# TensorE's eight expert passes of a mixture-of-experts block, written out one behind the other

## The chip, the cores and the metric

One Trainium2 chip, one core of it. The metric is the device time of one execution in microseconds; the time before is the median of three runs. The numbers of the profile come from one further execution, taken by the hardware profiler.

## The reference

Two small transformers stand one behind the other, in f32, on 256 tokens of width 1024 (and 256 context tokens beside them). The first has two hybrid layers (two kinds of attention and a convolution), the second a differential-attention layer with a dense feed-forward part, and then a Fourier-mixing layer with a mixture of experts. The change lies in that last part alone:

```python
def swiglu(h, w1, w3, w2):
    return (jax.nn.silu(h @ w1) * (h @ w3)) @ w2

def moe_swiglu(h, router, w1, w3, w2):          # 8 experts, D = 1024, D_FF = 3584
    logits = (h @ router).astype(jnp.float32)
    top_v, top_i = lax.top_k(logits, TOP_K)     # TOP_K = 2
    gates = jax.nn.softmax(top_v, axis=-1)
    ...                                         # rows sorted by expert
    def expert_block(args):
        xe, e = args
        return swiglu(xe, w1[e], w3[e], w2[e])
    yb = lax.map(expert_block, (xb, block_e))
    ...                                         # gated rows added up per token
```

Each expert has three f32 matrices of 1024 x 3584 numbers, 44 MB together, and is given the tokens that chose it.

## The kernel before

The kernel is written engine by engine, with semaphores set by hand: `block.sync` issues the loads, `block.tensor` the matmuls, `block.scalar` and `block.vector` work on what the matmuls leave in the eight banks of PSUM, `block.gpsimd` gathers and scatters rows by index. Everything before the experts (about the first 1,110 us) is straight code on every engine.

The experts are done in passes. A pass takes up to 96 tokens (`SLOTS`) of one expert. There are always eight passes, one for each expert, and up to five more (`OVER`) where an expert was chosen by more than 96 tokens. A list made on the chip (`LIST`) holds the number of all passes and of the extra ones. TensorE, ScalarE, VectorE and GpSimd each read the number of passes from it into a register (for TensorE line 1360) and run a loop of that many turns: lines 1362 (TensorE), 1882 (ScalarE), 2543 (VectorE), 727 (GpSimd). SyncE's loop over the eight experts (line 695) is separate from its loop over extra passes, which stands behind a test of `extra`.

A pass of TensorE consists of 24 chunks of weights in the order of `moe_order()`. The `up` chunks multiply the pass's tokens (`HE`, held in the memory of `modrow`) by columns of w1 or w3, and the `down` chunks multiply the hidden values by rows of w2. The order is: w1 first half, four chunks; `select(5)`, a small product that draws the rows of the next pass; w3 first half, four; w1 second half, four, with the transposes `turn_hidden(0)` after its second; `down(0, 0)` and `down(0, 1)`; w3 second half, four; `down(0, 2)`, `turn_hidden(1)`, `down(0, 3)`; `turn_tokens()`, which transposes the tokens of the next pass; and `down(1, 0)` to `down(1, 3)`. Nearly all products go through the helper `product`, so the profile puts them on its line, L757; the transposes are L1406 and L1416. One product of the source shows as two matmuls and two weight loads in the trace: a pass has 1,473 matmuls.

Chunks lie in a ring of eight slots in SBUF, 2 MB for a chunk of the first half and 1.5 MB for one of the second. SyncE loads a chunk (line 693) once TensorE has released its slot: `weights_used` is raised on the last matmul that reads the old chunk, or on one soon after it. TensorE waits for `weights_landed` before it reads a chunk (line 1370). It also waits for ScalarE and VectorE at places: before an `up` group for its bank (line 1388), before `select` for `pick_ready` (line 1441). That one is raised by VectorE (lines 2546 to 2555) at each pass's head: it waits until the last pass's result rows are scattered to DRAM (line 2548 behind GpSimd's line 735), and then makes the selection `PICK` for the next pass.

Every wait in the loop counts against the turn number `j`, as in

```python
pe.wait_ge(weights_landed[s], j * 48 + (landed_base[s] + 16 * (turn + 1)))
```

so the value waited for is worked out in a register in each turn. After the loop nothing is left for TensorE; ScalarE, VectorE and GpSimd then store the last result rows, fetch the two rows of each token, add them and apply the last norm.

Of the kernel before, what the change touches and what calls it, by code (L numbers as in the profile page):

```python
# [61 lines left out]
EXPERTS = 8  # L62
SLOTS = 96
GROUPS = SLOTS // 32
OVER = 5
# [133 lines left out]
def build(nc, a, table, out, dumps=None):  # L199
    chunks = weight_chunks(a)  # L200
    index = {}
    for i, (name, _) in enumerate(chunks):
        index.setdefault(name, []).append(i)
# [15 lines left out]
    for i, (_, parts) in enumerate(chunks):  # L219
        earlier.append(loads[slots[i]])  # L220
        loads[slots[i]] += 1
        total[slots[i]] += 16 * len(parts)
        landed_at.append(total[slots[i]])
    moe_slots = list(range(RING, LATE_SLOT)) + sorted(used_last, key=used_last.get) + [LATE_SLOT]

    with ExitStack() as ctx:
        def sb(name, shape, dt=F32):
            return ctx.enter_context(nc.sbuf_tensor(name, shape, dt))
# [146 lines left out]
        LIST = sb("LIST", [1, 32], I32)  # L375
        L_PASSES, L_EXTRA, L_OFFSET = 14, 15, 16
# [165 lines left out]
        def spec_columns(specs):  # L542

            at, c = [], 0
            for _, _, nb, n in specs:
                at.append(c)
                c += nb * (n // P)
            return at, c
# [3 lines left out]
        def moe_order():  # L552

            up = [[(w, st, q) for q in range(4)] for st in range(2) for w in ("w1", "w3")]
            down = [[("w2", st, q) for q in range(4)] for st in range(2)]
            return up[0] + up[1] + up[2] + down[0][:2] + up[3] + down[0][2:] + down[1]
# [191 lines left out]
        def _(pe):  # L748
# [424 lines left out]
            for what, u in attention_steps(2 * DA_HEADS, FILL[2]):  # L1173
# [3 lines left out]
                elif what == "scores":  # L1177
                    for i in range(2):
                        b, _ = start()
                        r = slice(64 * i, 64 * i + 64)  # L1180
# [176 lines left out]
            for primed in (silu_done, turned_ready, turned_taken, down_taken):  # L1357
                pe.sem_inc(primed, 3)
            pe.wait_ge(list_ready, 1)
            passes = pe.value_load(LIST[0:1, L_PASSES:L_PASSES + 1], min_val=EXPERTS, max_val=EXPERTS + OVER)  # L1360

            with pe.Fori(0, passes) as j:
                order = iter(enumerate(moe_order()))

                def moe_chunk(kind, st, q):
# [54 lines left out]
                def down(st, q):  # L1420

                    s, w = moe_chunk("w2", st, q)
                    rows = (4, 3)[st]
                    turned = HIDDEN_T[st]
                    if q == 0:
                        pe.wait_ge(turned_taken, j * 6 + (3 * st + 6))
                    for i in range(rows):
                        first, last = (st, q, i) == (0, 0, 0), (st, q, i) == (1, 3, rows - 1)

                        def part(g):  # L1430
                            return turned[:, q, i, 32 * g:32 * g + 32] if q < GROUPS else turned[:, g, i, SLOTS:P]

                        for r in range(GROUPS):
                            dst = bank[6 + r // 2][:, LAT * (r % 2):LAT * (r % 2) + LAT]
                            m = tiles(dst, part, part(r), w[:, i, :], LAT * r, LAT * GROUPS, first and r != 1,
                                      last and r != 0)
                    m.then_inc(weights_used[s], 1)
# [18 lines left out]
                for q in range(4):  # L1456
                    down(1, q)
                assert not release
            turn_log["pe"] = t.g


# [1164 lines left out]
```

## Time and profile before

| | |
|---|---|
| median of 3 runs | 2101.5 us (2100.93 to 2102.09) |
| the profiled execution's own time | 2105.07 us |
| its span, first to last instruction | 2103.2 us |
| mean granted TensorE clock in it | 0.965 |
| busy share: matmuls (PE) / weight loads (PEld) | 94% / 58% |
| busy share: VectorE / ScalarE / GpSimd | 35% / 27% / 1% |
| chain that ended last | PE 87%, DVE 5%, issue 3%, DMA 2%, ACT 2% |
| read from HBM / written | 535.19 MB / 5.25 MB |

Times in the profile are microseconds from the span's start. "Issue" is time in which an engine waited for nothing that the profile shows. PEq, DVEq and so on are an engine's sequencer, which handles branches, register arithmetic and waits and hands the rest on to the engine. Matmuls overlap each other, so their single durations are longer than the distance from one to the next. A granted clock of 1.00 is 2.4 GHz and one of 0.50 is 1.2 GHz.

### The profile page before, as it was taken

The numbers are of one execution on the slowest core, as the hardware profiler recorded it, in microseconds if no ns is written. First come the engines' busy times: TensorE is split into PE (matmuls) and PEld (weight loads), VectorE is DVE, ScalarE is ACT, GpSimd is POOL, SyncE is SP. The second block draws the span as 40 slices with busy tenths as digits, with TensorE's granted clock in tenths as the row PEclk, the third lists the DMA queues.
The fourth block names the chain that finished last, engine by engine and source line by source line (L and its number), as shares of the span: only waits on it lengthen the run. The fifth ranks groups of instructions, "written<-read, shape, count | busy, mean of one in ns | idle before, by whom it ended". The sixth has DMA issues, their size and how long they took to land.

```text
span 2103.2 us, 41141 instructions
## 1 busy us (share of the span) xinstructions
PE 1981.8 (94%) x18171; PEld 1218.5 (58%) x18171; DVE 736.7 (35%) x1419; ACT 576.4 (27%) x1062; POOL 27.6 (1%) x42
## 2 busy tenths in 40 slices
PE   6999998999899989999999989899999989999995
PEld 4785577866688467888873534435353443435343
DVE  4862756856744567665560000000000000000002
ACT  3233544444431555554440000000000000000001
POOL 1000000000000000000000000000000000000000
PEclk8999999999899999999999999999999999999998
DMA  9202522255632855566696999999999999989991
GB/s 328 83 33 99 201 81 67 101 202 189 250 120 81 322 186 212 181 204 181 230 382 242 393 348 374 387 341 411 332 395 347 376 380 352 409 329 393 349 370 69
DMA packets 179828, 543.29 MB, mean 258 GB/s; under 512 B 6778, under 2 KB 42257, under 8 KB 163132
## 3 DMA queue, kind: packets, MB, share of 16 engines
q1 hardware_dynamic: 175776, 528.63, 67.5%
q0 software_dynamic: 3104, 9.59, 1.3%
q8 instruction: 161, 2.64, 0.5%
q10 hardware_dynamic: 764, 2.24, 0.3%
q14 instruction: 23, 0.19, 0.0%
HBM read 535.19 MB, written 5.25 MB: 257 GB/s over the span
## 4 chain that ended last, share of the span: by engine, by line
PE 87%; DVE 5%; issue 3%; DMA 2%; ACT 2%; SPq 1%; POOL 0%; ACTq 0%; DVEq 0%; POOLq 0%; PEldq 0%
PE bank L757 82%; PE bank L795 2%; PE bank L1406 1%; DMA ring<-in_w_mod 1%; DVE ring_r L2104 1%; PE bank L866 1%; DMA ring<-in_ada_w 1%; SPq L686 1%; DVE nmax L2141 0%; PE bank L1070 0%; DVE H L2024 0%; DVE H_r L2033 0%; PE bank L827 0%; DVE H L2053 0%; ACT ring_r L1575 0%
## 5 line engine op out<-in xcount | busy, mean ns | idle before, releaser
L757 PE MATMUL bank<-scratch,modrow 128*32 128x384 f32 (+1 forms) x3840 | 380.5, 547 | 42.2 <-issue 42.0
L757 PE MATMUL bank<-H_r,ring_r 128*128 128x256 f32 (+2 forms) x1296 | 300.9, 314 | 1.4 <-ACT H_r L1486 1.4
L757 PEld LDWEIGHTS bank<-scratch,modrow 128*32 128x32 f32 x3840 | 130.9, 112 | 282.3 <-issue 282.3
L757 PE MATMUL bank<-scratch_r,ring_r 128*128 128x256 f32 (+2 forms) x1280 | 277.4, 344 | 5.6 <-ACT scratch_r L1559 2.1
L757 PE MATMUL bank<-ring,modrow 128*32 128x512 f32 (+1 forms) x2304 | 238.4, 557 | 0.0
L757 PEld LDWEIGHTS bank<-scratch_r,ring_r 128*128 128x128 f32 (+1 forms) x1280 | 216.4, 195 | 35.9 <-issue 4.6
L757 PEld LDWEIGHTS bank<-H_r,ring_r 128*128 128x128 f32 (+1 forms) x1296 | 222.9, 188 | 18.5 <-ACT H_r L1486 1.3
L757 PE MATMUL bank<-ring,scratch 128*32 128x256 f32 (+1 forms) x4048 | 228.0, 380 | 0.0
L2565 DVE TENSOR_TENSOR H<-H,bank 128x512 f32<-128x512 f32 (+1 forms) x48 | 29.8, 621 | 483.6 <-PE bank L757 483.6
L757 PE MATMUL bank<-H_r,scratch_r 128*128 128x512 f32 x544 | 192.7, 400 | 0.9 <-DVE H_r L2044 0.5
L757 PE MATMUL bank<-scratch 128*32 128x256 f32 (+5 forms) x2160 | 190.4, 370 | 2.8 <-ACT scratch L1481 1.8
L757 PEld LDWEIGHTS bank<-ring,scratch 128*32 128x32 f32 (+1 forms) x4048 | 132.3, 110 | 91.0 <-issue 6.0
L757 PEld LDWEIGHTS bank<-ring,modrow 128*32 128x32 f32 x2304 | 77.0, 110 | 143.9 <-issue 142.4
L1896 ACT ACTIVATE scratch<-bank 128x512 f32<-128x512 f32 (+1 forms) x48 | 22.6, 545 | 479.0 <-PE bank L1406 479.0
L757 PEld LDWEIGHTS bank<-scratch 128*32 128x32 f32 (+4 forms) x2160 | 109.7, 129 | 60.5 <-issue 31.2
L1481 ACT ACTIVATE scratch<-bank 128x512 f32<-128x512 f32 (+5 forms) x135 | 69.8, 530 | 194.3 <-PE bank L757 145.6
L757 PEld LDWEIGHTS bank<-H_r,scratch_r 128*128 128x128 f32 x544 | 102.8, 189 | 27.2 <-DVE H_r L2044 2.4
L2117 DVE TENSOR_TENSOR ring_r<-ring,scratch_r 128x2048 fp32r<-128x2048 f32 (+1 forms) x47 | 103.4, 2201 | 41.8 <-ACT scratch_r L1583 40.3
L2104 DVE TENSOR_TENSOR ring_r<-ring,ring_r 128x2048 fp32r<-128x2048 f32 (+2 forms) x42 | 92.4, 2200 | 25.1 <-ACT ring_r L1575 24.2
L1583 ACT ACTIVATE scratch_r<-ring 128x2048 fp32r<-128x2048 f32 (+1 forms) x47 | 86.1, 1836 | 41.6 <-PE bank L757 40.6
L1889 ACT ACTIVATE H<-bank 128x512 f32<-128x512 f32 (+1 forms) x48 | 26.1, 544 | 253.1 <-PE bank L757 253.1
L1575 ACT ACTIVATE ring_r<-ring 128x2048 fp32r<-128x2048 f32 (+2 forms) x42 | 77.3, 1841 | 60.7 <-PE bank L757 58.9
(249 smaller groups left out, 1692.4 us busy)
## 6 DMA issues: line engine op xcount, KB each, us to landing
ring<-in_moe_w SPq DMA_DIRECT2D x56, 2048.0 KB, 10.6
scratch<-in_moe_w SPq DMA_DIRECT2D x56, 1536.0 KB, 8.0
scratch<-in_moe_w SPq DMA_DIRECT2D x40, 2048.0 KB, 11.1
ring<-in_moe_w SPq DMA_DIRECT2D x40, 1536.0 KB, 9.3
ring<-in_ada_w SPq DMA_DIRECT2D x24, 2048.0 KB, 9.7
ring<-in_ff_w SPq DMA_DIRECT2D x14, 2048.0 KB, 7.8
ring<-in_w_mod SPq DMA_DIRECT2D x12, 2048.0 KB, 11.7
ring<-in_ff_w SPq DMA_DIRECT2D x8, 1792.0 KB, 8.2
```

What stands on the lines that cost most here:

```text
L686: sp.dma_start(dst, src).then_inc(weights_landed[s], 16)
L757: m = nc.tensor.matmul(out_, w, x_, start=first, stop=last)
L795: m = nc.tensor.transpose(dst, src, ident[0:n, 0:n])
L866: last = nc.tensor.matmul(bank[b][m * h:m * h + m, P * tt:P * tt + P], root[:, 3, c:c + 1].broadcast_to([P, m]), ident, start=True, stop=True)
L1481: nc.scalar.activation(dst, src, func, **kw).then_inc(bank_taken[b], 1)
L1575: nc.scalar.activation(high1(n), raw1(n, ring), ACT.Copy).then_inc(hi_ready, 1)
L1583: nc.scalar.activation(ff_high(n), ff_half(n, ring), ACT.Copy).then_inc(hi_ready, 1)
L1889: nc.scalar.activation(SIL[:, r, 0:WIDE[st]], bank[r][:, 0:WIDE[st]], ACT.Silu)\
L1896: nc.scalar.activation(HIDDEN_T[st][:, r, :, :], bank[3 + r][:, 0:WIDE[st]].rearrange("p (i s) -> p i s", s=P), ACT.Copy).then_inc(turned_ ...
L2104: v.tensor_tensor(raw1(n, ring_r), raw1(n, ring), high1(n).bitcast(F32), ALU.subtract)\
L2117: v.tensor_tensor(ff_half(n, ring_r), ff_half(n, ring), ff_high(n).bitcast(F32), ALU.subtract)\
L2565: v.tensor_tensor(HIDDEN[:, r, 0:WIDE[st]], SIL[:, r, 0:WIDE[st]], bank[3 + r][:, 0:WIDE[st]], ALU.mult).then_inc(mult_done, 1)
```

## The change

The body of TensorE's loop becomes a function `expert_pass(j)`. It is called eight times with the whole numbers 0 to 7, so that eight copies of the body stand one behind the other and the values waited for are constants. A ninth copy stands in a loop over the extra passes with `j = r + 8`, behind a test `extra > 0`. What is loaded into the register at line 1360 is now the number of extra passes. The inputs here give eight passes and no extra one. No matmul, no order and no wait's value is changed, and the other engines keep their loops.

```diff
             pe.wait_ge(list_ready, 1)
-            passes = pe.value_load(LIST[0:1, L_PASSES:L_PASSES + 1], min_val=EXPERTS, max_val=EXPERTS + OVER)
-
-            with pe.Fori(0, passes) as j:
+            extra = pe.value_load(LIST[0:1, L_EXTRA:L_EXTRA + 1], min_val=0, max_val=OVER)
+
+            def expert_pass(j):
+
                 order = iter(enumerate(moe_order()))
...
                 for q in range(4):
                     down(1, q)
                 assert not release
+
+            for e in range(EXPERTS):
+                expert_pass(e)
+            with pe.If(extra > 0):
+                with pe.Fori(0, extra) as r:
+                    expert_pass(r + EXPERTS)
+                pe.nop()
             turn_log["pe"] = t.g
```

## Rows read from the trace of the kernel before

**Rows 1.** The page: busy time by engine.
```profile
PE 1981.8 (94%) x18171; PEld 1218.5 (58%) x18171; DVE 736.7 (35%) x1419; ACT 576.4 (27%) x1062; POOL 27.6 (1%) x42
```

**Rows 2.** Waits of PE, 1110.3 to 2078.5 us: total us, times, longest us.
```profile
PE bank L757 <- issue: 42.0, 12, 5.3
```

**Rows 3.** The chain that ended last, in order of time: start us, us, what.
```profile
1110.60 51.30 PE bank L757 x484
...
1225.20 5.27 issue
1230.47 4.16 PE bank L757 x22
1234.63 1.33 issue
1235.96 47.95 PE bank L757 x462
...
1347.21 5.18 issue
...
1967.08 47.99 PE bank L757 x462
...
2078.41 0.02 issue
```

**Rows 4.** Sequencer, lines L1362, L1882, L1370, L1388: ns min/median/max, first and last start.
```profile
L1362 PEldq COMPARE_BRANCH  x8: 83/6082/6267, 1223.8 to 2077.0; - x8
...
L1882 ACTq COMPARE_BRANCH  x8: 40/45/59, 1225.3 to 2078.5; - x8
...
L1370 PEldq ALU_OP  x72: 32/32/32, 1125.1 to 2069.1; - x72
...
L1388 PEldq ALU_OP  x40: 32/32/42, 1110.7 to 2007.8; - x40
```

**Rows 5.** DMA queues, packets and MB: first 1225.2 to 1230.5 us, then 1230.5 to 1347.2.
```profile
DMA packets 285, 2.21 MB, mean 417 GB/s; under 512 B 16, under 2 KB 16, under 8 KB 16
q8 instruction: 1, 0.02, 1.3%
...
DMA packets 8022, 42.89 MB, mean 367 GB/s; under 512 B 400, under 2 KB 400, under 8 KB 6224
q8 instruction: 13, 0.21, 0.7%
```

**Rows 6.** Stretches: us, busy us (x) of PE, PEld, DVE, ACT, POOL, clock, DMA share, GB/s.
```profile
1595.90:1601.00 5.10, 5.07 (x22) 1.01 (x23) 0.00 (x0) 0.00 (x0) 0.00 (x0) 0.50 1.02 415
1602.00:1712.80 110.80, 110.80 (x1451) 49.55 (x1443) 4.62 (x12) 6.96 (x14) 0.92 (x1) 1.00 0.95 364
806.60:1096.80 290.20, 287.31 (x1732) 245.35 (x1730) 190.03 (x310) 151.66 (x233) 1.09 (x2) 1.00 0.67 226
1270.00:1347.00 77.00, 77.00 (x1145) 38.63 (x1137) 3.73 (x6) 5.17 (x11) 0.00 (x0) 1.00 1.01 398
```

**Rows 7.** Weight loads in order of time, start us and us of each four.
```profile
1236.39 0.15 PEld L757 LDWEIGHTS bank<-scratch,modrow 128*32 128x32 f32 x4 [0.27 <-issue]
1236.82 0.16 PEld L757 LDWEIGHTS bank<-scratch,modrow 128*32 128x32 f32 x4 [0.27 <-issue]
```

**Rows 8.** SyncE's waits, 1110 to 2079 us; landing of its loads, line L693.
```profile
SPq L693 <- PE bank L757: 857.2, 184, 31.9
...
DMA to landing us min/median/max: 6.2/9.6/23.6
```

**Rows 9.** VectorE in order of time at the second pass's head.
```profile
1236.92 0.15 DVE L2548 CAST result_row<-slot_next 96x1 int32<-96x1 f32 x1 [9.77 <-DMA result_rows<-scratch,result_row]
...
1238.88 0.16 DVE L2555 COPY of_slot<-of_expert 128x4 f32 x1
1255.47 0.15 DVE L2558 CAST slot_row<-bank 96x1 int32<-96x1 f32 x1 [16.43 <-PE bank L757]
```

## The prediction

> **What bounds the kernel now.** I read the page first. Matmuls are busy for 94% of the span, and no other engine for more than 35% [rows 1], so TensorE is the bound. From 1,110 us on there is nothing but the eight passes and, after 2078.41, a tail of 2103.2 - 2078.4 = 24.8 us in which TensorE does nothing [rows 3]. The question is then what TensorE waits for inside the passes. The list of its waits has one entry there: 42.0 us in 12 waits, the longest 5.3, and all for "issue", which is no semaphore, no other engine and no DMA [rows 2]. The chain of waits says where. A pass ends at 1225.20, TensorE stands for 5.27 us, runs 22 matmuls in 4.16 us, stands again for 1.33 us, and then goes through the pass with no further stop to 1347.21, where the next stall of 5.18 us begins [rows 3]. So the stall stands at the end of each turn of the loop, seven times in all. The end of the last pass, 2078.41, sets when the tail can begin.
>
> The stall has an owner. The loop's branch, line L1362, took 83 ns in one of its eight turns, the last (its start, 2077.0, is just before the last matmul), and about 6.1 us in the others, up to 6.27; the branches of ScalarE's loop took 40 to 59 ns [rows 4]. A branch that is not taken, and one in a short loop, cost next to nothing; a taken one in TensorE's long loop costs 6 us. The first begins at 1223.8, 1.4 us before the pass's end at 1225.20, because the sequencer runs ahead, so about 5 us of it are seen. The queues tell why: during the stall there is one packet of instructions (0.02 MB), and in the pass after it there are 13 with 0.21 MB, so 16 KB each [rows 5]. The body is fetched anew in every turn, and after the jump back TensorE has nothing to do until the first block is there. The 1.33 us after 22 matmuls have the look of the wait for the second block.
>
> **Skill and row.** The row says 6.1 us for a taken branch and 0.08 for the one not taken [rows 4]. The Trainium skill, "Advanced Engine Details and Errata", section Control Flow Timing, gives about 108 ns for a compare-and-branch, with no word of where it goes. By that figure seven branches would be worth 0.8 us in all and the change nothing; by the row each is worth fifty times as much. It is the second rival below, on a price of its own.
>
> **What the change removes.** *The seven jumps back.* Between one pass's last matmul and the next one's first there is now only the following instruction. I count what is lost at a turn as a whole, since the restart costs too: the clock. In 1595.9 to 1601 the granted clock is 0.50 (1.2 GHz), right behind such a stall, and 1.00 from 1602 to the pass's end [rows 6]. At 1.00 four matmuls of this kind start every 1236.82 - 1236.39 = 0.43 us, 0.107 each [rows 7], so 22 of them take 2.35 us where the turn shown needed 4.16 and then stood for 1.33.
> A pass from its 23rd matmul to its end takes 1347.21 - 1235.96 = 111.25 us, and in the last turn 2078.41 - 1967.08 = 111.33 [rows 3]. A pass with no stop in front is then 2.35 + 111.25 = 113.60. The seven passes after the first took 2078.41 - 1225.20 = 853.21 us with their stalls [rows 3]; written out they take 7 x 113.60 = 795.2. The difference is **58.0 us**. As a check, the shown turn lost 5.27 + 4.16 + 1.33 - 2.35 = 8.41, and the mean is 58.0 / 7 = 8.29. Of it some 5.1 is the branch and 3.2 the slow restart. The first pass (1110.60 to 1225.20 [rows 3]) is entered from straight code as before: 0.
>
> *The register arithmetic of the waits.* It runs in the sequencer ahead of the array, and a pass has no stop from it of its own [rows 2, 3]. I take 0. Nothing is added to the waits, so there is no loss. The most it could give back: lines L1370 and L1388 show 72 + 40 register operations of 32 ns in eight passes [rows 4], 14 a pass or 0.45 us; I allow 0.7 us a pass for these and the few of other waits, 8 x 0.7 = 5.6.
>
> **What it adds.** *The seam.* A pass's first matmuls wait for tokens, banks and a landed chunk; all have been raised before the pass ends, or the chain would show them behind the stall instead of issue [rows 3]. I take 0. The upper bound is 1 us at each of seven seams, an allowance for a short stop that the stall now hides. *The test for extra passes.* It jumps over a ninth body, once, so up to 6.27 us [rows 4]; it lies behind TensorE's last matmul and under the tail of 24.8 us, which does not use TensorE. With that cover gone it would cost 6.3. *The longer program.* Eight bodies are fetched once each instead of one body eight times: 13 packets a pass either way [rows 5].
>
> **What is late next.** Weights. A pass moves 2.21 + 42.89 = 45.1 MB [rows 5] in 121.9 us now, 370 GB/s, and in 113.6 it needs 397. The stretch 1270 to 1347, in which TensorE runs with no stop, has just that, 398 GB/s, and no wait for a load; in the stall 417 are moved [rows 5, 6]. SyncE is not behind: 184 of its loads in this part waited for TensorE to release a slot [rows 8]. A slot is loaded again about 8 of 24 chunks before its use, 8/24 of 113.6 = 38 us less the 5 us of the chunk itself; landing takes 9.6 us in the median and 23.6 at worst [rows 8]. That leaves 10 to 23 us. Next VectorE's selection for the following pass: it is done at 1239.04, 13.8 us after the pass's end, nearly all of it waiting for the scatter of result rows, and does not depend on TensorE's stall [rows 9]. TensorE's select ran just before VectorE's 1255.47 [rows 9], some 19 us after the 23rd matmul; written out it comes about 19 + 2.35 = 21.3 us after the old pass's end. The margin shrinks from 16 to 7.5 us. Both hold, so I cost them at 0, and they carry the first rival.
>
> **Sum.** The profiled execution: 2105.07 - 58.0 = 2047.1. It lies 3.6 us above the median of the runs, and nothing in the sum depends on that, so the forecast for the median is 2101.5 - 58.0 = **2043.5 us**. Its own bounds: 7 seams at 1 us above, and 5.6 us of register arithmetic below: 2037.9 to 2050.5.
>
> **Rivals.**
> 1. *The loads or the scatter become the wait.* For it: only 20 GB/s lie between what is needed and the most that is shown, and the stall now gives the queues a rest. Against: the 77 us at 398 GB/s. If the queues held 385 GB/s on average, a pass would be 45.1 / 385 = 117.1 us, 3.5 more, and 7 of them 25: 2068. Where VectorE's wait for the scatter took 10 us more than its 9.8, the cost would be 2.5 us a pass, 2061.
> 2. *The branch is cheap, and the stall has another cause that stays* (the next pass's operands, say). Then the seven branches are worth 0.083 us each [rows 4], 0.6 in all: 2100.9. By the page of the skill named above it would be this case. Against it: the branch's own duration holds the stall, and the one not taken has none [rows 4].
> 3. *The stop goes, the slow restart stays*, for instance by a second block that comes late at the seam. Then only the branches' 7 x 5.1 = 36 us go: 2065.5. Against: with no stop the clock has no cause to fall, and it stayed at 1.00 for 290 us of nearly unbroken matmuls before the passes [rows 6].
> 4. *Slower: straight code outruns its fetch.* If in the loop some of the 13 blocks were at hand from the turn before, written-out passes would stop at every block they now lack, 5.1 us each. The change then loses from 58.0 / (8 x 5.1) = 1.4 missed blocks a pass on; three a pass cost 8 x 3 x 5.1 = 122 us less 58: 2166. Against: the pass from 1110.60 was the first, with nothing at hand, and shows no stop; and 13 packets in a later pass are as many as 1,473 matmuls and as many weight loads fill, so none were kept [rows 3, 5].
>
> **How the numbers follow.** The forecast 0.86; rival 1 0.06; rival 3 0.04; rival 2 0.02; rival 4 0.02. No change that can be told is within 0.2%, 4.2 us, which only rival 2 gives; all of 1 and 3 is faster. So faster 0.96, same 0.02, slower 0.02. The range takes the forecast's own bounds, 2037.9 to 2050.5, a little outwards (the two readings of a pass differ by 0.08 us, 0.6 in seven, and the runs before spread over 1.2): 2036 and 2051. With 0.86 for the case and a little outside its bounds, that leaves out no more than 2 in 10; the other cases lie outside it.
>
> **What would show it.** In the chain of waits the 5 us "issue" entries at the passes' ends are gone, and passes follow each other at 113.6 us; TensorE's last matmul ends near 2020.4. The list of TensorE's waits keeps some 2 us of issue in this part. The granted clock is 1.00 from the first pass's start-up to the end. Instruction packets remain at 12 or 13 a pass. A wait of TensorE for a load or for VectorE's of_slot would show rival 1; a clock of 0.50 or a stop shortly after a seam rival 3; issue stops in mid-pass rival 4; an unchanged stop at the seams with another owner rival 2.

## The result, and the profile after

The changed kernel takes 2043.59 us (median of four runs, 2041.20 to 2045.51) against 2101.80 us for the kernel before beside it (2100.93 to 2105.25): a ratio of 0.9719, 95% interval 0.9705 to 0.9733. The forecast was 2043.5. The profiled execution took 2045.29 us, with a span of 2043.5.

The chain of waits of the changed kernel, in order of time (start us, us, what), shows two seams as nothing at all:

```profile
1112.23 1.50 issue
1113.73 51.41 PE bank L757 x484
...
1212.76 65.19 PE bank L757 x772
1277.95 1.46 PE bank L1407 x12
...
1325.57 65.19 PE bank L757 x772
1390.76 1.46 PE bank L1407 x12
...
2018.13 0.02 issue
```

The 288 matmuls that end a pass and the 484 that begin the next are now one piece, 772 matmuls in 65.19 us. Before they were 15.7 us, a stall of 5, 22 matmuls, a second stop and the other 462 [rows 3]. The same place of two successive passes (1277.95 and 1390.76) is 112.81 us apart; before it was 121.9 in the mean.

TensorE's waits from the first pass to the last (us in total, times, longest), against 42.0 us before [rows 2]:

```profile
PE bank L757 <- issue: 2.0, 1, 2.0
```

It is the stop ahead of the first pass. The branch at the passes' end is gone, and the test for extra passes, line L1463, took 3.8 us. It starts 1.5 us before TensorE's last matmul ends and lies under the tail for the rest:

```profile
L1463 PEldq COMPARE_BRANCH  x1: 3788/3788/3788, 2016.6 to 2016.6; - x1
```

The stretches (us, busy us of PE, PEld, DVE, ACT, POOL, granted clock, DMA share, GB/s) answer to [rows 6]:

```profile
1114.00:1117.40 3.40, 3.40 (x20) 1.08 (x16) 0.53 (x3) 0.00 (x0) 0.00 (x0) 0.50 0.02 5
1117.40:2018.00 900.60, 900.60 (x11768) 398.44 (x11760) 48.71 (x120) 72.62 (x140) 13.82 (x15) 1.00 0.96 381
```

The clock is 0.50 at the first pass's head and then 1.00 for 900 us of unbroken matmuls. DMA queues of one period, 1228.4 to 1341.2 us, the wait of SyncE's loads, and their landing time answer to [rows 5, 8]:

```profile
DMA packets 8305, 45.06 MB, mean 399 GB/s; under 512 B 416, under 2 KB 416, under 8 KB 6240
...
q8 instruction: 11, 0.18, 0.6%
```
```profile
SPq L693 <- PE bank L757: 793.5, 184, 31.7
```
```profile
DMA to landing us min/median/max: 6.3/10.8/23.8
```

The instruction packets are now 11 to 12 a pass, where the loop had 13 and one more at the turn. Loads land a little later (median 10.8 us, 9.6 before), and TensorE waits for none. VectorE's selection at the second pass's head answers to [rows 9]:

```profile
1241.88 0.17 DVE L2563 COPY of_slot<-of_expert 128x4 f32 x1
1249.51 0.15 DVE L2566 CAST slot_row<-bank 96x1 int32<-96x1 f32 x1 [7.46 <-PE bank L757]
```

The margin between the finished selection and the row that follows TensorE's select has gone from 16.4 to 7.5 us.

**Where the time came from.** The two profiled executions differ by 2105.07 - 2045.29 = 59.8 us. From the first matmul of the passes to the last it was 2078.41 - 1110.60 = 967.8 us and is 2018.13 - 1113.73 = 904.4: 63.4 less. The part ahead of the passes was 3.1 us longer in this execution, and the tail 0.5 (25.3 for 24.8): 63.4 - 3.1 - 0.5 = 59.8.

### The profile page after: what moved, and what is told of

Its sections match the earlier page's. It is cut to its first block, busy times and chain, and to the rows that moved or that the text cites. A ratio compares the mean times of both kernels' runs of the same rounds, so it can differ in the third digit from the quotient of the medians.

```text
span 2043.5 us, 40941 instructions
## 1 busy us (share of the span) xinstructions
PE 1960.7 (96%) x18171; PEld 1213.8 (59%) x18171; DVE 737.0 (36%) x1419; ACT 576.5 (28%) x1062; POOL 27.5 (1%) x42
## 4 chain that ended last, share of the span: by engine, by line
PE 89%; DVE 5%; DMA 2%; ACT 2%; issue 1%; SPq 1%; POOL 0%; ACTq 0%; DVEq 0%; POOLq 0%; PEldq 0%
PE bank L757 83%; PE bank L795 2%; PE bank L1407 1%; DMA ring<-in_w_mod 1%; PE bank L866 1%; DVE ring_r L2112 1%; DMA ring<-in_ada_w 1%; DVE nmax L2149 1%; SPq L686 1%; PE bank L1070 1%; DVE H L2032 0%; DVE H_r L2041 0%; PE bank L827 0%; ACT ring_r L1583 0%; DVE scratch L1999 0%
## 5 line engine op out<-in xcount | busy, mean ns | idle before, releaser
L757 PE MATMUL bank<-scratch,modrow 128*32 128x384 f32 (+1 forms) x3840 | 358.3, 531 | 2.0 <-issue 2.0
L757 PEld LDWEIGHTS bank<-scratch,modrow 128*32 128x32 f32 x3840 | 125.3, 110 | 224.5 <-issue 223.3
L757 PE MATMUL bank<-ring,modrow 128*32 128x512 f32 (+1 forms) x2304 | 232.8, 557 | 0.0
L2578 DVE SCALAR_TENSOR_TENSOR scratch<-bank,slot_gate,X 96x512 f32<-96x512 f32 (+1 forms) x16 | 9.1, 610 | 219.3 <-PE bank L757 219.3
## 6 DMA issues: line engine op xcount, KB each, us to landing
ring<-in_w_mod SPq DMA_DIRECT2D x12, 2048.0 KB, 11.7
```

Of the source, the lines that this page charges most:

```text
L757: m = nc.tensor.matmul(out_, w, x_, start=first, stop=last)
```

## The experiments

Each is an edit of the changed kernel. The theory is that a jump back over a body which TensorE no longer holds costs a fetch, and then a restart. Rivals are the register arithmetic of the waits, and any taken branch on TensorE.

### Four turns of two bodies

```diff
-            for e in range(EXPERTS):
-                expert_pass(e)
+            with pe.Fori(0, EXPERTS // 2) as pair:
+                expert_pass(pair * 2)
+                expert_pass(pair * 2 + 1)
```

Expected: 

> TensorE's passes in a loop of four turns with two bodies each, in place of eight bodies: three taken jumps back instead of seven or none. If each taken jump back over a long body costs its stall and restart (63.4 us less in the passes for seven jumps, 9.1 each, or 8.3 by the working of the prediction), the time is 25 to 27 us above the straight kernel, 2068.5 to 2071. If the gain came from constants in place of register values (this kernel still waits on register values in every pass), it stays near the kernel before, 2101. If a longer body makes the stall longer, over 2075.

Measured: 2070.14 us (2068.27 to 2070.26), ratio to the kernel before 0.9843, 0.9829 to 0.9856. The three turns are all that TensorE waits for, and they look like the old ones. Chain, then the branch's row:

```profile
1335.67 5.98 issue
1341.66 5.34 PE bank L757 x22
1347.00 0.09 issue
...
1442.66 65.19 PE bank L757 x772
```
```profile
L1461 PEldq COMPARE_BRANCH  x4: 83/6872/7067, 1334.3 to 2041.2; - x4
```

The seam inside the body (the 772 matmuls from 1442.66) costs nothing, with register values in every wait. In the trace the places where such a piece of 772 begins are 235.5, 235.4 and 236.0 us apart, which is 9.8 to 10.4 us more than two straight passes (2 x 112.81). The time agrees: it is 27.6 us above the next experiment's 2042.56, which has register values and no jump, or 9.2 a jump, and 29.3 above the straight kernel's 2040.88 (below, from another group of runs), or 9.8. The looped kernel lost 63.4 / 7 = 9.1 a jump. The branch itself was 0.8 us longer here (6.87 for 6.08), so the loss goes with the number of jumps, with a slightly dearer stall whose cause is open.

### Register values with no jump

```diff
+            zero = pe.value_load(LIST[0:1, 0:1], min_val=0, max_val=EXPERTS - 1)
...
-                expert_pass(e)
+                expert_pass(zero + e)
```

Expected: 

> Eight bodies written out, but each pass's number is a register (a zero loaded once, plus a constant), so that all waits are again against values worked out in registers, with no jump. Theory of the jump: no change against the straight kernel, 2043.6 within 1 us, plus the one load of some 0.5 us before the passes. Rival, the register arithmetic was what made a warm pass 113.6 us where it is now 112.8: 0.8 us a pass more, 2049 to 2050, with passes 113.6 us apart in the chain.

Measured: 2042.56 us (2041.68 to 2047.40), ratio 0.9720, 0.9707 to 0.9733. The register operations are back and the passes do not feel them. Line L1373 (L1370 in [rows 4]), then the chain:

```profile
L1373 PEldq ALU_OP  x72: 32/32/32, 1125.8 to 2006.3; - x72
```
```profile
1275.37 1.46 PE bank L1409 x12
...
1322.99 65.19 PE bank L757 x772
1388.18 1.46 PE bank L1409 x12
```

1388.18 - 1275.37 = 112.81 us again. The register arithmetic is worth nothing, and it is not what made the prediction's pass 113.6 us.

### A near jump back at every seam

```diff
             for e in range(EXPERTS):
+                if e:
+                    with pe.Fori(0, 2):
+                        pe.nop()
                 expert_pass(e)
```

Expected: 

> Eight bodies written out, and at each of the seven seams a loop of two turns around one empty instruction: seven taken jumps back on TensorE, over a body of a few instructions. Theory of the far jump: 0.1 us of sequencer time each, hidden by the queue in front of the array, 2043.6 within 1 us, and the branch's row shows under 0.1 us. Rival, any taken jump on TensorE throws the fetched instructions away: 5 to 8 us each, 2079 to 2102.

Measured: 2039.78 us (2036.22 to 2041.42), ratio 0.9699, 0.9686 to 0.9713; passes again 112.81 us apart. Seven of the 14 branches below are taken, and none took over 0.26 us (under 0.1 was expected):

```profile
L1463 PEldq COMPARE_BRANCH  x14: 76/145/253, 1220.8 to 1898.0; - x14
```

A taken jump by itself costs TensorE nothing here. So it is the far one.

### How far is far: bodies of growing length

A first try with empty instructions (`pe.nop()`) as the filling settled nothing.

Expected: 

> The straight kernel, and behind its passes on TensorE six loops of three turns over 128, 448, 960, 1,472, 1,984 and 2,496 empty instructions, so that each loop's own branch can be read. If what counts is the distance jumped back against what TensorE still holds, the branch costs under 0.1 us up to some length and about 4 to 6 us (3.8 in the last branch of the straight kernel, with quiet queues) from there on, with the edge between 448 and 2,496. If every jump back of more than a block of 256 costs, 448 and longer all show it. The total time is not compared.

The loop over "2,496" of them took as long as that over "128": the three branches of each start some 0.4 us apart, so nothing stood in the bodies. (Its one run took 2038.88 us.) The branches of the "2,496":

```profile
L1477 PEldq COMPARE_BRANCH  x3: 76/207/213, 2019.7 to 2020.4; - x3
```

The second try used matmuls of four columns:

```diff
+            def filler():
+                nc.tensor.matmul(bank[3][:, 0:4], ident, tab[:, T_ONES:T_ONES + 4], start=True, stop=True)
+
+            with pe.Fori(0, 3):
+                for _ in range(32): filler()
...
+            with pe.Fori(0, 3):
+                for _ in range(624): filler()
```

Expected: 

> The empty instructions of the last try of this kind left nothing in the program. Now six loops of three turns over 32, 112, 240, 368, 496 and 624 small matmuls stand behind the passes, each matmul some four instructions as the trace counts them. Theory of the distance: the taken branch of the short bodies costs 0.1 to 0.3 us and that of the long ones 3.4 to 4 us with quiet queues (3.4 to 3.9 in the test for extra passes), with one edge somewhere from 112 to 624. Rival, the cost grows evenly with the length. The total time is not compared.

And a third closed in on the edge.

Expected: 

> The edge more closely: six loops of three turns over 384, 416, 432, 448, 464 and 480 small matmuls, 1,536 to 1,920 instructions, between the 1,472 whose jump back cost 0.2 us and the 1,984 whose jump cost 3.6 to 3.9. If TensorE holds what it last ran up to some length, there is one edge and every body past it costs. If what counts is where blocks of 256 instructions (16 KB) begin, two neighbouring lengths can differ the other way round, or one loop's two jumps can differ.

One run of each, 4415.26 and 5376.62 us. The branch rows (ns min/median/max of three, of which the last, some 76, isn't taken), first 368 and 496 matmuls of the second try, then 384 and 416 of the third:

```profile
L1477 PEldq COMPARE_BRANCH  x3: 76/207/208, 2661.2 to 2975.3; - x3
L1479 PEldq COMPARE_BRANCH  x3: 76/3574/3880, 3186.9 to 3610.4; - x3
```
```profile
L1471 PEldq COMPARE_BRANCH  x3: 76/222/240, 2175.6 to 2503.3; - x3
L1473 PEldq COMPARE_BRANCH  x3: 76/3427/3509, 2680.8 to 3035.8; - x3
```

One turn of the 368 shows as 736 matmuls and as many weight loads, so a matmul of the source is four instructions:

```profile
2504.30:2661.20 156.90, 156.90 (x737) 156.90 (x737) 0.00 (x0) 0.00 (x0) 0.00 (x0) 0.50 0.00 1
```

Every body up to 1,536 instructions jumped back in 0.21 to 0.24 us, every one from 1,664 up in 3.4 to 3.9 us, with no growth from there to 2,496. In these two runs it is one edge. A pass has 2 x 1,473 = 2,946 matmuls and loads, well past it. The branch takes 3.4 to 3.9 us while the DMA queues are quiet, and 6.0 to 6.3 in the looped kernel, where they run full. In the loop over two passes (5,892 matmuls and loads a turn) it took 6.8 to 7.1, and no run tells whether that is the length.

The duration of the branch is not yet what TensorE loses. From 2026.5 to 4409 us of the second try there are four jumps of 3.5 to 3.9 us, and TensorE was busy for 2382.36 of the 2382.50 us (the row stands in the last section): matmuls that were already handed on filled the time. In the looped kernel only the first 1.4 us of the branch were covered in this way, and the other 5 were seen.

The Trainium skill, "Runtime: NRT & Kernel Launch", section Instruction fetch mechanics, says that a taken branch forces a fetch when its target lies outside the current window of two 16 KiB pages. The trace agrees on the fetch and the 16 KB packets [rows 5], and not on the window: two such pages are 512 instructions, and a jump over 1,536 was free.

### A stop without a jump, at the seam

```diff
             for e in range(EXPERTS):
+                if e:
+                    pe.wait_ge(result_stored, e * 16 + 16)
                 expert_pass(e)
```

Expected: 

> Eight bodies written out; at each of the seven seams TensorE waits until the last pass's result rows are scattered, a stop of some 11.7 us without a jump. It parts the restart's two causes. If the slow restart (3.2 us, or 4.0 with what the prediction missed) is the clock alone, a seam costs the stop plus 3 to 4 us. If the clock gives about 2 us (the first 20 or so matmuls at twice 0.107) and the second block's stop and the tiles' lost step gave the rest, a seam costs the stop plus 1.5 to 2.2 us, there is no second stop, and a pass from its 23rd matmul on is 110.4 to 110.5 us, as in the straight kernel, and not 111.25. Time: 2043.6 + 7 x (11.7 + 2) = 2139, or 2147 to 2153 by the first.

Measured: 2133.51 us (2126.81 to 2138.84), ratio 1.0152, 1.0135 to 1.0169. Chain at one seam, then the clock around the restart:

```profile
1352.38 0.04 issue
1352.42 52.22 PE bank L757 x484
```
```profile
1347.40:1357.40 10.00, 4.98 (x24) 1.19 (x28) 0.68 (x4) 0.00 (x0) 0.00 (x0) 0.50 0.73 303
1357.60:1460.00 102.40, 102.40 (x1311) 43.84 (x1307) 3.95 (x8) 6.97 (x14) 0.93 (x1) 1.00 0.94 355
```

TensorE's stop was 10.4 us at this seam (74.0 us in seven, where 11.7 each was expected, and so the time lies under the 2139 expected). There is no second stop: the 484 matmuls run in one piece, and the tiles keep in step (next experiment). The unbroken ones take 65.19 - 15.68 = 49.5 us, so this restart lost 2.7, all with a clock of 0.50. From period to period, less 112.81 and the stop, it was 2.3 to 3.1 us, more than the 1.5 to 2.2 expected, as the clock stayed at 0.50 longer here (5.0 us of matmuls at it above). So a stop of ten microseconds with no jump costs 2.3 to 3.1 us more at the restart, with the granted clock at 0.50; and the second stop belongs to the jump.

In the kernel before, that second stop hides the slow clock. From a pass's first matmul to its 23rd it took 5.2 to 5.7 us after each of the seven jumps, whether the 22 matmuls needed 4.16 us and the stop 1.33 [rows 3] or, at the last turn, nearly all of it went into the matmuls:

```profile
1961.65 5.34 PE bank L757 x22
1966.99 0.08 issue
```

Here, with the clock at 0.50 too, it is 4.28 us, and in the straight kernel 2.16. So about 1 us of a restart in the kernel before is not the clock. That it is the wait for the second block of instructions is the likely reading, not shown.

### A stop in the middle of a group of four tiles

```diff
-                def tiles(dst, own, other, w, column, last_column, first, last):
+                def tiles(dst, own, other, w, column, last_column, first, last, hold=False):
...
+                    if hold:
+                        pe.wait_ge(result_stored, j * 16 + 16)
                     return product(dst[P - 32:P, :], other, w[:, last_column:last_column + dst.shape[-1]], first, last)
```

`hold` is set for the twelfth product of a pass after the first, so the stop falls behind 22 matmuls.

Expected: 

> Written-out passes, and in each of the last seven a wait for the scattered result rows after the 22nd matmul, in the middle of a group of four tiles, where the looped kernel had its second stop. Theory of the lost step: the four tiles run side by side, and a stop after two of a group leaves each later group shifted, which comes due where select needs all of them: from the 97th matmul to select it takes 0.4 to 0.8 us more than in the kernel with the wait at the seam, at the same clock of 1.00, and VectorE's slot_row follows later by as much. If 0.8 us of the looped pass came from register arithmetic or the fetch, there is no such difference (the kernel with register values and no jump had none).

Measured: one run, 2110.43 us. Weight loads just ahead of `select` (the 128x96 ones, whose time includes the idle before them), with the stop in the group, with the stop at the seam, and in the kernel before:

```profile
1371.32 0.11 PEld L757 LDWEIGHTS bank<-ring,modrow 128*32 128x32 f32 x1 [0.31 <-issue]
1371.75 0.11 PEld L757 LDWEIGHTS bank<-ring,modrow 128*32 128x32 f32 x1 [0.32 <-issue]
1372.69 0.41 PEld L757 LDWEIGHTS bank<-of_slot,pick 128*96 128x96 f32 x4 [0.84 <-issue]
```
```profile
1374.27 0.12 PEld L757 LDWEIGHTS bank<-ring,modrow 128*32 128x32 f32 x4 [0.31 <-issue]
1374.70 0.12 PEld L757 LDWEIGHTS bank<-ring,modrow 128*32 128x32 f32 x4 [0.31 <-issue]
1375.66 0.41 PEld L757 LDWEIGHTS bank<-of_slot,pick 128*96 128x96 f32 x4 [0.84 <-issue]
```
```profile
1253.56 0.11 PEld L757 LDWEIGHTS bank<-ring,modrow 128*32 128x32 f32 x1 [0.27 <-issue]
1253.99 0.11 PEld L757 LDWEIGHTS bank<-ring,modrow 128*32 128x32 f32 x1 [0.32 <-issue]
1254.93 0.41 PEld L757 LDWEIGHTS bank<-of_slot,pick 128*96 128x96 f32 x4 [0.84 <-issue]
```

Four tiles of 32 columns normally start together every 0.43 us. In the first and the third kernel two such steps ahead of `select` start one load each: the tiles have slipped against each other and finish one by one. From a pass's 97th matmul to its `select` it is 11.24 us here, 11.21 in the kernel before, 10.40 with the stop at the seam and 10.41 with none. That is 0.8 us lost ahead of `select`. It is not all net: from the 23rd to the 97th matmul, at a clock of 1.00, the looped kernel takes 7.76 us and the straight one 8.14, since the shifted groups gain 0.38 us first. So the slip costs a pass 0.4 us. Where a stop falls in a group of tiles matters, up to the next instruction that needs them all.

### Less matmul work, all loads

```diff
-                    for i in range(rows):
+                    for i in (0, rows - 1):
```

Expected: 

> Two of four rows of each first-half down chunk and one of three of each second-half one are left out of the products (288 of a pass's 1,473 matmuls, 15.5 us); all loads stay. It shows how far the loads are from being the bound. If they have room, a pass falls towards 112.8 - 15.5 = 97.3 us, 1935 in all; at the 417 GB/s seen during the stalls 45.1 MB take 108 us, so the loads should become the bound at 106 to 109 us a pass, 1990 to 2015 in all, with waits of TensorE for moe_w. If the loads were already all but the bound (the first rival), a pass stays above 111 us, over 2030.

Measured: 1992.19 us (1991.15 to 1993.24). The kernel leaves out products, so its result is wrong; only its time is of use. Waits of TensorE over six passes, and one period's stretch:

```profile
PE bank L757 <- DMA ring<-in_moe_w: 33.5, 37, 2.1
PE bank L757 <- issue: 14.7, 6, 3.3
PE bank L757 <- DMA scratch<-in_moe_w: 14.2, 17, 1.5
```
```profile
1415.80:1525.70 109.90, 99.27 (x1185) 40.04 (x1185) 6.40 (x16) 9.35 (x19) 1.82 (x2) 1.00 1.02 412
```

With 15.5 us less to compute a pass shrinks by only 2.9, to 109.9 us (106 to 109 was expected), and TensorE waits for weights in 54 places. The six waits named "issue" stand at the passes' ends, where there is no jump, and they are loads too: each ends 0.1 us after the next pass's first chunk has landed (at 1415.72 us for the matmul of 1415.81, and so for the other five). A load now takes 26.5 us in the median to land, where it took 10.8. The total came within the expected range with the help of the first two passes, which ran on chunks loaded ahead and took 97.3 and 105.1 us.

The queues are full for the whole period and carry 412 GB/s. So the straight pass of 112.8 us stands 2.6% above what these loads allow: what TensorE could still save beyond 2.9 us a pass would buy nothing.

### The load of the number of extra passes, moved behind the passes

```diff
-            pe.wait_ge(list_ready, 1)
-            extra = pe.value_load(LIST[0:1, L_EXTRA:L_EXTRA + 1], min_val=0, max_val=OVER)
...
             for e in range(EXPERTS):
                 expert_pass(e)
+            pe.wait_ge(list_ready, 1)
+            extra = pe.value_load(LIST[0:1, L_EXTRA:L_EXTRA + 1], min_val=0, max_val=OVER)
             with pe.If(extra > 0):
```

Expected: 

> The wait for the list and the load of the number of extra passes are moved behind the eight written-out passes, where alone they are needed. The 1.5 us of issue between TensorE's last wait before the passes and its first matmul of them go: 1.3 to 1.8 us less than the straight kernel, 2042 to 2042.3. If the first pass's slow start at the half clock shrinks too, up to 1 us more, 2041. Rival: the wait on wide_taken before it ends last in any case and the load was hidden: 2043.6.

Measured: 2036.84 us (2035.76 to 2038.38), ratio 0.9687, 0.9674 to 0.9701. No plain straight kernel ran beside it; both follow on one chip.

Expected of the straight kernel: 

> The changed kernel once more, on the same chip as the kernel with the late load, so that the two can be set against each other. 2038 to 2044, with passes 112.81 us apart; what varies between executions lies ahead of the passes.

Expected of the late load: 

> The late load once more, beside the straight kernel. In its trace the stop ahead of the first pass was 1.1 us in place of 2.0 and the first pass took 112.8 us in place of 114.5, as the clock was 1.00 from its start. If these two are the gain, it is 2.5 us, some 0.12%. If the lower time seen was the part ahead of the passes that varies by itself, the two are within 1 us.

Measured: 2040.88 us (2034.59 to 2041.57) for the straight kernel, ratio 0.9702, 0.9688 to 0.9715; 2038.57 us (2036.31 to 2040.04) for the late load, ratio 0.9689, 0.9676 to 0.9702. The chains at the first pass's head, straight kernel, late load, and the kernel with the stop at the seam, which has the load in its old place:

```profile
1101.60 1.51 issue
1103.11 51.41 PE bank L757 x484
```
```profile
1107.64 0.65 issue
1108.29 49.72 PE bank L757 x484
```
```profile
1101.14 1.54 issue
1102.68 49.72 PE bank L757 x484
```

The stop is 0.86 us shorter, and the traces show that much of a gain. The 484 matmuls are 1.69 us shorter than in the straight kernel, but that is not the late load's doing: 49.72 us also stand in the traces of five kernels that load the number early (the one shown, and those with the stop in the group, less matmul work, empty bodies and the third try of bodies), and 51.2 to 52.5 in the other six. The clock at the first pass's head varies from one execution to the next. Whether the late load makes the full clock more likely, two traces cannot tell. The difference of the medians is 2.3 us, the intervals overlap, and the start of the passes alone differs by 5 us the other way in these two executions (1103.1 and 1108.3), so the times do not tell the gain from none. It is the version with the lowest median, and it beats the kernel before beyond doubt.

## Why the prediction was right

The time (2043.5 forecast, 2043.59 measured) is closer than the working deserves; two misses of a few microseconds cancelled in the profiled execution (5.5 us more gained in the passes, 3.6 lost ahead of and behind them), and the same kernel's median in the other group of runs is 2040.88. That it came within 0.1 us is luck.

- **The stall has an owner, the taken branch over the long body.** Right, and now shown from both sides: no jump, no stall (with register values as well as constants); three far jumps, three stalls; seven near jumps, none. The loss goes with the number of far jumps.
- **The slow restart goes with the stall.** Right. Behind the first pass's head the clock is 1.00 to the end. With a stop but no jump the restart still cost 2.3 to 3.1 us. That the second stop after 22 matmuls is the wait for the second block is consistent (it comes with the jump and not with a mere stop); it was not shown by itself.
- **58.0 us for seven turns.** This term was too small. A pass was taken as 113.60 us; it is 112.81, and the passes gained 63.4 us. The step that failed is "a pass with no stop in front is then 2.35 + 111.25", a sum of pieces read off an interrupted pass. Single starts of matmuls in the traces divide its 0.79 us into three. The 23rd matmul starts 2.16 us after the first, not 2.35, as it belongs to the group of four that begins with the 21st. At an unbroken seam the next pass's first matmul starts 0.19 us before the recorded end of the last one, which pieces on two sides of a stall can't show. And the tiles out of step lose 0.80 us ahead of `select`, of which they had gained 0.38 before. That makes 0.2 + 0.2 + 0.4, and 7 x 0.79 = 5.5 us is the difference to 63.4. The bound of a gain through register arithmetic covered its size but named a wrong cause.
- **Seam, register arithmetic, test for extra passes, longer program: 0.** Right, though the packets were not "13 a pass either way": the loop had 14 with the one at the turn, and there are now 11 or 12. The 772 matmuls over a seam take 65.19 us in every pass; the test's 3.8 us cost nothing that can be seen.
- **Weights and selection next, with a margin.** Right: no wait for either. The margin of the selection was forecast at 7.5 us and is 7.5. The margin of the loads was read from the wrong place, though. They were judged by lead and by the 417 GB/s seen in a stall; what they can sustain is 412, a pass of 109.9 us, so the bandwidth's margin was 2.6%. The rival of the loads was nearer than 6 in 100 suggests.
- **Own time against the median.** The 3.6 us between profiled execution and median before became 1.7 after. What varies is the part ahead of the passes: the first pass began at 1113.7 us in one profiled execution of the straight kernel and at 1103.1 in the other, while its passes were 112.81 us apart in both.

The rivals: the cheap branch (2100.9) is refuted by the time itself; the slow restart that stays, and the straight code that outruns its fetch, by the chain, which has no stop in 900 us.

## What to carry to other kernels

An "issue" wait that stands at the end of every turn of a long loop can be the instruction fetch of the jump back: look for the duration of the branch instruction itself, and compare the turn that isn't taken. Then take the jump away to be sure, since here "issue" also stood for a load, and branches of 3.5 us left TensorE busy. On TensorE write the body out, or keep it to the 1,536 instructions of the trace that jumped back freely here (a f32 matmul of the source counts as four). When pricing a stall, add what it leaves behind (the lower clock, tiles out of step), and find the next bound by taking work away from the engine, not by the highest rate seen in a lull.

## What the runs showed of the hardware that was not expected

- TensorE jumps back over up to 1,536 instructions in 0.24 us and over 1,664 to 2,496 in 3.4 to 3.9 us; under full DMA queues, over 2,946 and 5,892 matmuls and loads, it is 6.0 to 7.1.
- In the runs with small matmuls the granted clock stayed at 0.50 for all of 2,382 us in which TensorE ran matmuls of four columns with no idle time:

```profile
2026.50:4409.00 2382.50, 2382.36 (x11168) 2382.19 (x11168) 9.01 (x14) 5.62 (x9) 0.00 (x0) 0.50 0.00 1
```

- A stop in the middle of a group of four 32-column tiles costs 0.8 us later, at the next instruction that needs all columns, with no wait in any list (0.4 us net, with what the shifted groups gain before it).
